# Fetching the first two samples' index pages from the stage before, by SyncE alone

## The chip, the cores and the metric

The kernel runs on one core of one Trainium2 chip. The metric is the device time of one execution in microseconds (us); lower is better. Times shown as a position ("at 1081.97") count from the first instruction of the profiled execution.

## The reference, cut to what matters

One inference step of a two-layer decoder trunk, for one prompt of 512 tokens and eight samples of one new token each, whose 2048 past tokens lie in caches cut into pages of 128 tokens. The part at hand is the indexer of layer 0, which scores the tokens and keeps the best of them; for a sample the keys of the past come through its page table:

```python
def dsa_select(qi, wi, kidx, t, topk):
    dots = jnp.einsum('bqhd,bld->bqhl', qi, kidx, preferred_element_type=jnp.float32) * (D_IDX ** -0.5)
    score = jnp.einsum('bqh,bqhl->bql', wi.astype(jnp.float32), jax.nn.relu(dots))
    s = jnp.arange(kidx.shape[1])
    score = jnp.where(s[None, None, :] <= t[None, :, None], score, NEG)
    return lax.top_k(score, topk)[1]
# in att_sample:
ki_all = jnp.concatenate([gather_pages(c_idx_k, page_table), ki], axis=1)
idx = dsa_select(qi, wi, ki_all, t, topk)
```

There are 16 index heads of 128 numbers; a sample has 16 pages of 128 x 128 float32, 64 KB each.

## The kernel before

The program is a row of stages. Each stage is a block in which every engine (TensorE, VectorE, ScalarE, GpSimd and SyncE, here PE, DVE, ACT, POOL and SP) runs its own list of instructions, ordered by semaphores. At the end of a stage GpSimd clears the stage's semaphores and all five engines meet in a barrier: the next stage starts when the last of them has come. Two stages matter here, and a third that follows.

**The prompt's block (stage_rows_and_index).** First it turns ten tiles of projections into rows for the outputs. Then it scores the prompt: a loop over the 16 index heads, two to a turn. SP fetches a head's queries into one of two buffers when the matmuls that read the buffer before are done (the DMA of line 741), PE multiplies them with the keys (line 767), ACT applies the relu (line 798), DVE adds the weighted result to the mask (line 836). Behind the loop DVE prepares the samples' queries (lines 846 to 850), and POOL cuts the mask (line 862). SP's last act in this block is one DMA of 4 MB, the weights of the next-but-one stage (load_w1, line 880), into the buffer k.w. The page table is loaded early in this block, under the semaphore table_in.

**The samples' index (stage_index_sample).** PE first clears four banks and adds the new token's own logits (lines 912 and 914); neither needs a page. Then, sample by sample, it turns the 16 pages (turn_keys, line 923, in four groups of four pages that DVE copies out, line 969), and one sample later multiplies the sample's queries with the turned keys (add_logits, line 930). So the order is: turn 0, turn 1, add 0, turn 2, add 1, turn 3 and so on. The pages lie in two buffers, of the even and the odd samples. SP fetches pages 0 to 7 of each sample and ACT pages 8 to 15, with the helper load_pages: it reads eight page numbers into registers and then issues eight DMAs of 64 KB (line 875). Ahead of each group both wait until the buffer's last sample has been turned:

```python
sp.wait_ge(turned, j * 8 + (4 * b + 4))
load_pages(k, sp, k.i["cache_dsa_idx_k"], pg[:, b, 0:8], arrived[b], j * 2 + b, 0, 8)
```

PE starts by adding 8 to the semaphore turned, so that the first two samples' fetches go at once when the stage starts. PE waits in turn_keys for all 16 pages of a sample on the semaphore arrived.

**The compression (stage_compress)** comes next; its line 1028 is the first to read the 4 MB in k.w.

Of the kernel before, what the change touches and what calls it, by code (L numbers as in the profile page):

```python
# [19 lines left out]
P = 128  # L20
# [4 lines left out]
NS = 8  # L25
# [7 lines left out]
PG = 16  # L33
# [660 lines left out]
def stage_rows_and_index(k):  # L694
# [11 lines left out]
    with ExitStack() as ctx:  # L706
# [11 lines left out]
        with nc.Block() as block:  # L718

            @block.sync  # L720
            def _(sp):
                for n, (tile, name) in enumerate(tiles):
                    if n >= 2:

                        sp.wait_ge(turned, n - 1)
                    if parts(name) == 2:
                        sp.dma_start(src[:, n % 2, :, :], k.proj[tile:tile + 2].rearrange("g p c -> p g c")).then_inc(tile_in[n % 2], 16)
                    else:
                        sp.dma_start(src[:, n % 2, 0, :], k.proj[tile]).then_inc(tile_in[n % 2], 16)
                    if n == 1:  # L730
                        sp.dma_start(k.pages[:, :], k.i["page_table"].rearrange("(o s) p -> o (s p)", o=1)).then_inc(table_in, 16)
                        sp.dma_start(k.hot[:, :], k.i["hot"][:, T:O_ALL]).then_inc(table_in, 16)
                        sp.dma_start(k.sT[:, :, :], k.proj[0:GW, :, T:TC].rearrange("t p s -> p t s")).then_inc(got, 16)
                sp.dma_start(ki[:, :], k.proj[KI]).then_inc(k_in, 16)

                sp.wait_ge(gated, 2)
                sp.dma_start(k.gate_rows, k.gws[:, :]).then_inc(out, 16)
                with sp.Fori(0, NI // 2) as j:
                    for b in range(2):
                        sp.wait_ge(mm_done, j * 2 + (b + 1))  # L740
                        sp.dma_start(q[:, b, :], k.proj[bass.ds(j * 2 + (QI + b), 1)].rearrange("o p c -> (o p) c")).then_inc(q_in[b], 16)
                load_w1(k, sp, "k")
                sp.wait_ge(table_in, 32)

            @block.tensor
            def _(pe):
# [131 lines left out]
def load_w1(k, eng, which):  # L878

    eng.dma_start(k.w1[which], k.i["cmp_w1_" + which][0].rearrange("(l d) n -> d l n", d=P)).then_inc(k.w1_in[which], 16)  # L880


def stage_index_sample(k):

    nc, ps = k.nc, k.psum
    arrived = [k.sem("is_arrived0"), k.sem("is_arrived1")]
    turned, kept, used, qcopy, relu_done, summed, scored, step = (k.sem(f"is_{n}") for n in
        ("turned", "kept", "used", "qcopy", "relu", "summed", "scored", "step"))
    with ExitStack() as ctx:
        pg = k.sb("is_pages", [P, 2, PG, P], ctx=ctx)  # L890
        kt = k.sb("is_keys", [P, 2, PAST], ctx=ctx)
        qs = k.sb("is_q", [P, 2, P], ctx=ctx)
        rl = k.sb("is_relu", [P, PAST + 1], ctx=ctx)
        sc = k.mask_s
        with nc.Block() as block:

            @block.sync
            def _(sp):
                with sp.Fori(0, NS // 2) as j:
                    for b in range(2):  # L900

                        sp.wait_ge(turned, j * 8 + (4 * b + 4))
                        load_pages(k, sp, k.i["cache_dsa_idx_k"], pg[:, b, 0:8], arrived[b], j * 2 + b, 0, 8)
                load_w1(k, sp, "v")

            @block.tensor
            def _(pe):
                pe.sem_inc(turned, 8)
                pe.sem_inc(used, 2)
                pe.sem_inc(kept, 2)  # L910
                for c in range(4):
                    pe.matmul(ps[:, c, :], k.zeros[:, :], k.xT[:, 0, 0:512], start=True, stop=True)
                for s in range(NS):
                    mm = pe.matmul(ps[:, 4, 0:1], k.qpi[:, s * P:(s + 1) * P], k.sT[:, KI, s:s + 1], start=(s == 0), stop=(s == NS - 1))
                mm.then_inc(summed, 1)

                def turn_keys(j2, s):
                    pe.wait_ge(arrived[s % 2], (j2 + s - s % 2) * (8 * PG) + 16 * PG)
                    for c in range(4):

                        pe.wait_ge(kept, j2 * 4 + (4 * s + c + 1))
                        for g in range(4):
                            mm = pe.transpose(ps[:, 5 + c % 2, g * P:(g + 1) * P], pg[:, s % 2, c * 4 + g, :], k.ident)
                        mm.then_inc(turned, 1)

                def add_logits(j2, s):
                    pe.wait_ge(qcopy, j2 + (s + 1))
                    pe.wait_ge(kept, j2 * 4 + (4 * s + 6))
                    for c in range(4):
                        mm = pe.matmul(ps[:, c, :], qs[:, s % 2, :], kt[:, s % 2, c * 512:(c + 1) * 512], start=False, stop=True, skip_group_check=True)  # L930
                    mm.then_inc(used, 1)

                turn_keys(0, 0)
                with pe.Fori(0, NS // 2 - 1) as j:
                    for s in range(2):

                        turn_keys(j * 2, s + 1)
                        add_logits(j * 2, s)
                turn_keys(0, NS - 1)
                add_logits(0, NS - 2)  # L940
                add_logits(0, NS - 1)
                pe.wait_ge(relu_done, 5)
                for c in range(4):
                    mm = pe.matmul(ps[0:NS, c, :], k.wsel[:, :], rl[:, c * 512:(c + 1) * 512], start=True, stop=True)
                pe.matmul(ps[0:NS, 4, 0:1], k.wsel[:, :], rl[:, PAST:PAST + 1], start=True, stop=True).then_inc(scored, 1)

            @block.scalar
            def _(act):
                with act.Fori(0, NS // 2) as j:
                    for b in range(2):  # L950

                        act.wait_ge(turned, j * 8 + (4 * b + 4))
                        load_pages(k, act, k.i["cache_dsa_idx_k"], pg[:, b, 8:16], arrived[b], j * 2 + b, 8, 8)
                act.wait_ge(used, NS + 2)
                act.wait_ge(summed, 1)
                for c in range(4):
                    nc.scalar.activation(rl[:, c * 512:(c + 1) * 512], ps[:, c, :], ACT.Relu).then_inc(relu_done, 1)
                nc.scalar.activation(rl[:, PAST:PAST + 1], ps[:, 4, 0:1], ACT.Relu).then_inc(relu_done, 1)

            @block.vector  # L960
            def _(dve):
                with dve.Fori(0, NS // 2) as j:
                    for b in range(2):

                        dve.wait_ge(used, j * 2 + (b + 1))
                        dve.tensor_copy(qs[:, b, :], k.qpi[:, bass.ds(j * 256 + b * P, P)]).then_inc(qcopy, 1)
                        for c in range(4):
                            dve.wait_ge(turned, j * 8 + (8 + 4 * b + c + 1))
                            dve.tensor_copy(kt[:, b, c * 512:(c + 1) * 512], ps[:, 5 + c % 2, :]).then_inc(kept, 1)
                dve.wait_ge(scored, 1)  # L970
                dve.tensor_copy(sc[:, 0:PAST], ps[0:NS, 0:4, :].rearrange("p b c -> p (b c)"))
                dve.tensor_copy(sc[:, PAST:PAST + 1], ps[0:NS, 4, 0:1]).then_inc(step, 2)
                dve.wait_ge(step, 2)
# [1419 lines left out]
def build(nc, ins, outs):  # L2393
    with ExitStack() as ctx:
        k = Kernel(nc, ctx, ins, outs)
# [13 lines left out]
        k.gate_rows = k.dram("gate_rows", [NS, NGW])  # L2409
        k.w_free = [k.sem(f"w_free{s}") for s in range(4)]  # L2410
        k.y_out = [k.sem(f"y_out{b}") for b in range(2)]
        k.w_in = [k.sem(f"w_in{s}") for s in range(4)]
        k.w1_in = {which: k.sem("w1_in_" + which) for which in "kv"}

# [4 lines left out]
        with ExitStack() as layer0:  # L2419
# [20 lines left out]
            with ExitStack() as sample:  # L2440
# [4 lines left out]
                with ExitStack() as compressing:  # L2445

                    k.w1 = {"k": k.w[:, :, :].rearrange("p s (l n) -> p (s l) n", n=CH), "v": k.sb("w1_v", [P, CB, CH], ctx=compressing)[:, :, :]}
                    with ExitStack() as indexing:
                        k.qpi = k.sb("qpi", [P, NS * P], ctx=indexing)
                        k.zeros = k.sb("zeros", [P, P], ctx=indexing)  # L2450
                        with k.stage():
                            stage_rows_and_index(k)
                        with k.stage():
                            stage_index_sample(k)
                    with k.stage():
                        stage_compress(k, "k")
                    with k.stage():
                        stage_compress(k, "v")
# [69 lines left out]
```

## Time and profile before

| what | value |
|---|---|
| time, median of 3 runs | 3264.4 us (3262.85 to 3266.66) |
| the profiled execution's own time | 3262.51 us |
| its span, first to last instruction | 3260.9 us |
| share of the span in which PE, DVE, ACT and POOL are busy | 90%, 42%, 22%, 4% |
| mean granted TensorE clock | 0.943 of full |
| prompt's scoring, first to last matmul of line 767 | 1027.1 to 1073.3 |
| samples' index, first matmul of line 912 to last of line 945 | 1081.3 to 1147.4 |

Between the end of the last instruction and what the time counts lie 1.6 us. The profile is of one execution, and the three runs lie 3.8 us apart.

### The profile page before, as it was taken

What the parts mean: (1) busy time and instruction counts of PE and PEld (TensorE: products, weight loads), DVE (VectorE), ACT (ScalarE), POOL (GpSimd) and SP (SyncE); (2) the same over time, 40 slices, a digit from 0 to 9 for tenths busy, and PEclk for the clock granted to TensorE, in tenths of its full rate; (3) what the DMA queues carried; (4) which work ended last, traced back from release to release, by engine and by line L of the source; (5) the groups of instructions that cost most, each with busy time, mean ns of one, the idle gap of its engine ahead of it and who ended that gap; (6) DMA issues with size and microseconds to landing.
All of it is one profiled execution on the core that took longest, in us unless ns stands there. A gap on an engine that the chain in (4) does not pass through costs nothing. (4 is left out here: it accounts for less than half of the span.)

```text
span 3260.9 us, 56498 instructions
## 1 busy us (share of the span) xinstructions
PE 2934.2 (90%) x22144; PEld 2601.3 (80%) x22144; DVE 1365.2 (42%) x2213; ACT 710.9 (22%) x1085; POOL 131.6 (4%) x150
## 2 busy tenths in 40 slices
PE   7699999999995789798888896797999999999897
PEld 3499999999983468688544464797999999999897
DVE  2422242222344447566562476434444334433434
ACT  2211222111221122121000254322322222222222
POOL 0000030000130000000000000000000000000000
PEclk8799999999997999899897698898999999999998
DMA  9766567676646733231889524632233333333421
GB/s 334 234 194 193 176 197 229 219 233 215 179 130 164 219 117 98 78 93 45 262 266 348 172 85 153 179 91 80 80 98 86 103 97 97 96 94 113 117 79 52
DMA packets 594874, 496.87 MB, mean 152 GB/s; under 512 B 37148, under 2 KB 515885, under 8 KB 593885
## 3 DMA queue, kind: packets, MB, share of 16 engines
q1 hardware_dynamic: 527912, 408.44, 42.5%
q10 hardware_dynamic: 58992, 60.59, 5.7%
q0 software_dynamic: 7840, 26.10, 2.1%
q8 instruction: 82, 1.34, 0.2%
q14 instruction: 48, 0.39, 0.0%
HBM read 460.02 MB, written 48.70 MB: 156 GB/s over the span
## 5 line engine op out<-in xcount | busy, mean ns | idle before, releaser
L146 PE MATMUL psum<-h_high,w_high 128*128 128x260 f32 x4992 | 1009.3, 283 | 21.6 <-DVE w_low L133 21.6
L146 PE MATMUL psum<-h_high,w_low 128*128 128x260 f32 x4992 | 1007.0, 283 | 0.0
L146 PE MATMUL psum<-h_low,w_high 128*128 128x260 f32 x4992 | 1005.2, 283 | 0.0
L146 PEld LDWEIGHTS psum<-h_high,w_high 128*128 128x128 f32 x4992 | 770.7, 189 | 35.9 <-issue 30.1
L146 PEld LDWEIGHTS psum<-h_high,w_low 128*128 128x128 f32 x4992 | 770.8, 189 | 0.0
L146 PEld LDWEIGHTS psum<-h_low,w_high 128*128 128x128 f32 x4992 | 768.9, 189 | 0.0
L133 DVE TENSOR_TENSOR w_low<-w,w_high 128x2048 fp32r<-128x2048 f32 x162 | 371.7, 2296 | 560.5 <-ACT w_high L128 560.5
L128 ACT ACTIVATE w_high<-w 128x2048 fp32r<-128x2048 f32 x162 | 309.1, 1909 | 473.3 <-PE psum L146 361.3
L628 DVE COPY pj_out<-psum 128x260 f32<-128x260 f32 x66 | 28.3, 429 | 380.3 <-PE psum L146 380.3
L576 ACT ACTIVATE pj_out<-psum 128x260 f32<-128x260 f32 x66 | 25.6, 387 | 583.3 <-PE psum L146 583.3
L199 PE MATMUL psum<-w,c 128*32 128x512 f32 x768 | 104.8, 659 | 26.1 <-DMA w<-in_w_ada 17.5
L1041 PE MATMUL psum<-w,cz_xtk 128*128 128x256 f32 x512 | 117.3, 391 | 0.0
L1041 PE MATMUL psum<-w_v,cz_xtv 128*128 128x256 f32 x512 | 117.1, 390 | 0.0
L1041 PEld LDWEIGHTS psum<-w,cz_xtk 128*128 128x128 f32 x512 | 115.4, 309 | 0.5
L1041 PEld LDWEIGHTS psum<-w_v,cz_xtv 128*128 128x128 f32 x512 | 115.3, 308 | 0.4
L1583 DVE COPY at_kt<-psum 128x512 f32<-128x512 f32 x144 | 93.0, 686 | 34.9 <-PE psum L1383 34.6
L2069 DVE TENSOR_TENSOR ou_t<-psum,adaT 128x8 f32<-128x8 f32 x32 | 5.3, 165 | 197.8 <-PE psum L146 187.0
L2351 DVE RECIPROCAL cv_parts<-cv_parts 128x520 f32<-128x520 f32 x16 | 54.5, 3404 | 71.9 <-ACT cv_parts L2285 71.9
L199 PEld LDWEIGHTS psum<-w,c 128*32 128x32 f32 x768 | 20.0, 114 | 71.3 <-issue 40.5
L166 PE MATMUL psum<-h_high,w_high 128*128 128x260 f32 x192 | 41.9, 301 | 34.2 <-DVE h_low L2036 22.4
L632 DVE RECIPROCAL pj_ez<-pj_ez 128x520 f32<-128x520 f32 x16 | 54.5, 3403 | 40.3 <-POOL pj_ez L664 40.3
L669 POOL DMA_DIRECT2D proj<-pj_out x66 | 36.7, 556 | 735.3 <-DVE pj_out L628 727.5
(372 smaller groups left out, 2772.1 us busy)
## 6 DMA issues: line engine op xcount, KB each, us to landing
w<-in_w_ada SPq DMA_DIRECT2D x96, 1024.0 KB, 7.7
w<-in_w_in_att SPq DMA_DIRECT2D x65, 1024.0 KB, 11.3
w<-in_w_in_conv SPq DMA_DIRECT2D x64, 1024.0 KB, 6.2
proj<-pj_out POOLq DMA_DIRECT2D x66, 260.0 KB, 4.8
cz_pgk<-in_cache_nsa_cmp_k SPq DMA_DIRECT2D x128, 128.0 KB, 2.1
cz_pgv<-in_cache_nsa_cmp_v SPq DMA_DIRECT2D x128, 128.0 KB, 2.1
w<-in_w_out_att SPq DMA_DIRECT2D x16, 1024.0 KB, 6.2
w<-in_w_out_conv SPq DMA_DIRECT2D x16, 1024.0 KB, 6.0
```

The lines of the kernel that those rows point to most:

```text
L128: act.activation(k.wh[:, s % 2, :], k.w[:, n % 4, :], ACT.Copy).then_inc(self.high, 1)
L133: dve.tensor_tensor(k.wl[:, s % 2, :], k.w[:, n % 4, :], k.wh[:, s % 2, :].bitcast(F32), ALU.subtract).then_inc(k.w_free[n % 4], 1)
L146: mm = pe.matmul(k.psum[:, banks + hf, 0:HC], w[:, kt, :], x[:, kt, hf * HC:(hf + 1) * HC], start=(kt == 0 and m == 0), stop=(kt == KT - 1 ...
L166: mm = pe.matmul(k.psum[:, banks[i] + hf, 0:HC], w[:, kt, :], x[:, kt, hf * HC:(hf + 1) * HC], start=(kt == 0 and m == 0), stop=(kt == KT ...
L199: mm = pe.matmul(k.psum[32 * a:32 * a + 32, self.bank, :], k.c32[:, q * 4 + a, :], k.w[:, n % 4, a * 512:(a + 1) * 512], start=(q == 0), s ...
L576: nc.scalar.activation(out[:, t % 4, 0:HC], ps[:, t % 2 * 2, 0:HC], ACT.Copy).then_inc(kept_a, 1)
L628: dve.tensor_copy(out[:, t % 4, HC:TC], ps[:, t % 2 * 2 + 1, 0:HC]).then_inc(kept_v, 1)
L632: dve.reciprocal(ez[:, t % 2, :], ez[:, t % 2, :]).then_inc(zrec, 1)
L669: pool.dma_start(to, out[:, t % 4, :]).then_inc(stored[t % 4], 16)
L1041: mm = pe.matmul(ps[:, b, 0:CH], rows, w1[:, l, :], start=(l == 0), stop=(l == CB - 1))
L1583: dve.tensor_copy(kt[:, s % 2, :, c * 256:(c + 1) * 256], ps[:, 3 + q % 2, :].rearrange("p (g q) -> p g q", g=G)).then_inc(kept, 1)
L2351: dve.reciprocal(e[:, :], e[:, :]).then_inc(zrecip, 1)
```

## The change

SP now fetches all 16 pages of samples 0 and 1 in the prompt's block: 32 DMAs in four groups, in straight-line code between its last query and load_w1, which moves behind them. The wait for the page table moves ahead of them. In the samples' stage the loops of SP and of ACT begin with the second pair of samples, so ACT fetches nothing for samples 0 and 1 any more. The page buffer is_pages and its two arrival semaphores now live across both stages.

```diff
@@ stage_rows_and_index, sync
                         sp.dma_start(q[:, b, :], k.proj[bass.ds(j * 2 + (QI + b), 1)].rearrange("o p c -> (o p) c")).then_inc(q_in[b], 16)
+                sp.wait_ge(table_in, 32)
+                for b in range(2):
+                    for half in range(0, PG, 8):
+                        load_pages(k, sp, k.i["cache_dsa_idx_k"], k.is_pages[:, b, half:half + 8], k.is_arrived[b], b, half, 8)
                 load_w1(k, sp, "k")
-                sp.wait_ge(table_in, 32)
@@ stage_index_sample
-    arrived = [k.sem("is_arrived0"), k.sem("is_arrived1")]
+    arrived = k.is_arrived
...
-        pg = k.sb("is_pages", [P, 2, PG, P], ctx=ctx)
+        pg = k.is_pages
@@ sync
-                with sp.Fori(0, NS // 2) as j:
+                with sp.Fori(1, NS // 2) as j:
@@ scalar
-                with act.Fori(0, NS // 2) as j:
+                with act.Fori(1, NS // 2) as j:
@@ build
+        k.is_arrived = [k.sem(f"is_arrived{b}") for b in range(2)]
...
+                        k.is_pages = k.sb("is_pages", [P, 2, PG, P], ctx=indexing)
```

## Rows read from the trace of the kernel before

**Rows 1.** Page, part 1: busy us (share of the span) and instructions.
```profile
PE 2934.2 (90%) x22144; PEld 2601.3 (80%) x22144; DVE 1365.2 (42%) x2213; ACT 710.9 (22%) x1085; POOL 131.6 (4%) x150
```

**Rows 2.** Timeline, all engines, 1066 to 1082: start, length, engine and line [idle before].
```profile
1065.83 2.50 SPq L741 DMA_DIRECT2D ip_q<-proj  x2
...
1068.60 4.71 PE L767 MATMUL psum<-ip_k,ip_q 128*128 128x128 f32 x16 [0.80 <-DMA ip_q<-proj]
1068.63 0.39 SPq L880 DMA_DIRECT2D w<-in_cmp_w_k  x1
...
1079.65 0.22 DVE L850 TENSOR_SCALAR wsel<-const,wi_s 128x8 f32<-128x8 f32 x1
1081.20 0.23 DVE L966 COPY is_q<-qpi 128x128 f32 x1 [1.33 <-PEq L909]
...
1081.27 1.19 PE L912 MATMUL psum<-xT,zeros 128*128 128x512 f32 x1 [7.95 <-PEq L102]
```

**Rows 3.** Timeline, PE alone, 1086 to 1101: the first three turnings.
```profile
1086.28 1.84 PE L914 MATMUL psum<-sT,qpi 128*128 128x1 f32 x16
1088.52 1.09 PE L923 MATMUL psum<-const,is_pages 128*128 128x128 f32 x8 [0.40 <-DMA is_pages<-in_cache_dsa_idx_k]
1089.96 1.25 PE L923 MATMUL psum<-const,is_pages 128*128 128x128 f32 x8 [0.35 <-DVE is_keys L969]
1093.55 1.09 PE L923 MATMUL psum<-const,is_pages 128*128 128x128 f32 x8 [2.34 <-DMA is_pages<-in_cache_dsa_idx_k]
1094.99 1.97 PE L923 MATMUL psum<-const,is_pages 128*128 128x128 f32 x8 [0.35 <-DVE is_keys L969]
1096.75 4.20 PE L930 MATMUL psum<-is_keys,is_q 128*128 128x512 f32 x8
1100.79 0.38 PE L923 MATMUL psum<-const,is_pages 128*128 128x128 f32 x2
```

**Rows 4.** Timeline, SP alone, single page fetches of samples 0, 1 and 2.
```profile
1081.97 0.34 SPq L875 DMA_DIRECT2D is_pages<-in_cache_dsa_idx_k  x1
...
1085.59 0.33 SPq L875 DMA_DIRECT2D is_pages<-in_cache_dsa_idx_k  x1
1086.84 0.33 SPq L875 DMA_DIRECT2D is_pages<-in_cache_dsa_idx_k  x1
...
1092.04 6.06 SPq L875 DMA_DIRECT2D is_pages<-in_cache_dsa_idx_k  x9
```

**Rows 5.** Timeline, SP alone, 1552 to 1574: 32 page fetches without a loop.
```profile
1554.30 8.70 SPq L875 DMA_DIRECT2D w<-in_cache_nsa_slc_k  x16
1563.73 9.94 SPq L875 DMA_DIRECT2D at_slots<-in_cache_nsa_slc_k  x16
1573.72 0.36 SPq L1296 DMA_DIRECT2D at_vn<-out_slc_v_s  x1
```

**Rows 6.** The same, single fetches: eighth of group one, first of group two.
```profile
1557.92 0.33 SPq L875 DMA_DIRECT2D w<-in_cache_nsa_slc_k  x1
1558.99 0.33 SPq L875 DMA_DIRECT2D w<-in_cache_nsa_slc_k  x1
```

**Rows 7.** DMA issues of the span: queue, count, KB each, median us to landing.
```profile
w<-in_cmp_w_k SPq DMA_DIRECT2D x1, 4096.0 KB, 15.7
is_pages<-in_cache_dsa_idx_k ACTq DMA_DIRECT2D x64, 64.0 KB, 2.3
is_pages<-in_cache_dsa_idx_k SPq DMA_DIRECT2D x64, 64.0 KB, 2.1
...
w<-in_cache_dsa_v SPq DMA_DIRECT2D x32, 128.0 KB, 9.9
```

**Rows 8.** Busy time by stretch (PE, PEld, DVE, ACT, POOL), then PE's granted clock, DMA share, GB/s.
```profile
1076.00:1080.00 4.00, 0.00 (x0) 0.00 (x0) 3.87 (x35) 0.00 (x0) 1.08 (x4) 0.69 1.10 348
1080.00:1084.00 4.00, 2.73 (x4) 1.22 (x5) 0.23 (x1) 0.00 (x0) 0.00 (x0) 0.50 0.86 267
1084.00:1086.00 2.00, 2.00 (x6) 1.01 (x5) 0.00 (x0) 0.00 (x0) 0.00 (x0) 0.92 0.90 251
1094.60:1097.90 3.30, 2.95 (x11) 2.40 (x11) 2.31 (x4) 0.00 (x0) 0.00 (x0) 0.50 0.76 218
1100.79:1106.70 5.91, 5.56 (x26) 3.18 (x25) 2.80 (x5) 0.00 (x0) 0.00 (x0) 1.00 0.54 153
```

**Rows 9.** Timeline, 1100 to 1210: the first read of the 4 MB.
```profile
1153.74 6.42 PE L1028 MATMUL psum<-w,cz_petk 128*32 128x256 f32 x64 [0.29 <-ACT cz_petk L1092]
```

## The prediction

> **What bounds the kernel now.** Read the shares of the engines first: PE is busy 90% of the span [rows 1], and no other engine half of it. The kernel is mostly a matmul stream, so time can be won or lost here only where PE stands idle, and those places are read one by one. The timeline around the seam between the two stages shows one: the last matmul of line 767 ends at 1073.31 (1068.60 + 4.71), and PE's next, of line 912, starts at 1081.27 [rows 2]. Nothing about pages holds it there. What holds it is the barrier, and the last to come is DVE, which ends line 850 at 1079.87; 1.33 us later the next stage runs. SP came long before: it ended its 4 MB issue at 1069.02. So SP has 1079.87 - 1069.02 = 10.85 us of slack in the prompt's block, and that is all the cover there is.
>
> Next, PE alone after the seam. The page waits can be seen directly: 0.40 us ahead of turn 0 and 2.34 us ahead of turn 1, both released by the fetch of is_pages [rows 3]. From turn 2 on one sample takes 5.91 us with the clock at 1.00 [rows 8], and PE waits for DVE's copies, not for pages. The whole price of the late pages is therefore 2.74 us, plus what the clock adds: the second half of turn 1 takes 1.97 us where the same of turn 0 took 1.25, and the granted clock there, 1094.6 to 1097.9, is 0.50, the lower of its two levels (1.2 GHz), after PE had stood idle from 1091.21 to 1093.55 [rows 3, 8].
>
> **The change, part by part.** *Loop bounds and semaphores.* ACT loses 16 DMAs and SP's stage-two loop 16; both engines then wait for turn 0, as they did for sample 2 before. Nothing on PE, DVE or POOL changes its own list.
>
> *The 32 fetches on SP.* First their pace. Eight fetches of one group start at 1081.97 to 1085.59, so 3.62 / 7 = 0.517 us each, and a group lasts 3.62 + 0.33 = 3.95 us [rows 4]. Then the register reads between groups: 0.92 us in the loop (1085.92 to 1086.84) [rows 4], 0.74 us in straight-line code (1558.25 to 1558.99) [rows 6]. Straight-line groups start 4.72 us apart: (1563.73 - 1554.30) / 2 [rows 5]. The change's code is straight-line, so I take 0.74 and 4.72.
>
> SP's last query issue ends at 1068.33, and 0.30 us later the old block issued its 4 MB [rows 2]. The first page then starts at 1068.33 + 0.30 + 0.74 = 1069.37; the fourth group at 1069.37 + 3 x 4.72 = 1083.53 and ends at 1087.48. The wait for the page table costs nothing, being met since the block's start. The 4 MB issue follows 0.05 us later (as line 1296 follows the pages [rows 5]) and takes 0.39: SP is done at 1087.92. DVE's end was 1079.87. **The barrier moves by 8.05 us.** Bounds: without the 0.30 and at 4.69, 7.6; if 32 fetches take 19.37 us from first to last, as those of [rows 5] did (1554.30 to 1573.67; 128 KB pages with ACT fetching too), 9.3 us.
>
> The Trainium skill, DMA: Bandwidth & Descriptors, section Issuing engines are not separate DMA queues, says that issuing from several engines saves only the sequencer's time of issue, "which is usually small relative to the DMA itself". By that word the fold onto one engine would be nearly free and the sum would be the 3.0 us of gain below. The rows disagree for this size: 32 issues at 0.517 us are 16.5 us of SP's time.
>
> *What becomes earlier after the barrier.* I count from turn 0's start, t0. Lines 912 and 914 keep their 1081.27 to 1088.12; the clock has already fallen to 0.50 at the seam [rows 8], and a longer idle time finds it no lower. Then turn 0 starts at once: 0.40 saved. Before, turn 2 started at t0 + 12.27 (1088.52 to 1100.79 [rows 3]). After, two things must be ready. PE: turn 0 takes 2.69 and turn 1 with add 0 the steady 5.91, so t0 + 8.60; or, if the clock still falls at that place, 12.27 - 2.34 = 9.93. Sample 2's pages: they can be asked for only when turn 0 is over (2.69), their first issue follows 0.83 later (1091.21 to 1092.04, [rows 3, 4]), the eighth starts 3.62 on, and 2.1 (SP) to 2.3 (ACT) later it has landed [rows 7]: t0 + 9.2 to 9.5. So **a new wait of up to 0.9 us stands ahead of turn 2** in place of the 2.34, or the lower clock does. Turn 2 starts at 9.5 or 9.9; the gain is 0.40 + 2.8, or 0.40 + 2.3: 2.7 to 3.2, I take 3.0. At best (pages no limit, no fall of the clock) it is 0.40 + 3.67 = 4.1. Sample 3 is not late: SP's next group starts at 2.69 + 0.83 + 3.95 + 0.92 = 8.4 and has landed by 8.4 + 3.62 + 2.3 = 14.3, turn 3 needs it at 9.5 + 5.91 = 15.4.
>
> *The 4 MB, moved behind 32 DMAs.* Issued at 1087.5 and not 1068.63, it lands 15.7 us later [rows 7], at 1103.2. Its reader comes at 1153.74 [rows 9], so it is not late itself. But its transfer, covered before by the prompt's last heads, now meets sample 2's fetches. With turn 0 at 1088.12 + 8.05 = 1096.2, these are issued from 1099.7 to 1103.6: the 4 MB is nearly through, and the last page, which sets the wait, is issued after it has landed. I take nothing. At worst a page lands as late as those of in_cache_dsa_v, 9.9 us [rows 7]; turn 2 then starts at 2.69 + 0.83 + 3.62 + 9.9 = 17.0, a loss of 4.7 - 0.40 = 4.3 instead of the gain.
>
> **Sum.** +8.05 - 3.0 = **+5.0 us**. Every engine passes the barrier and no later stage sees more than a shift. Bounds without a collision: 7.6 - 4.1 = +3.5 to 9.3 - 2.7 = +6.6. The profiled execution's 3262.5 (span 3260.9 and 1.6 around it) becomes 3267.5; it lies 1.9 below the median of the runs, by which it would be 3269.4. As the result is a median, I give 3269.
>
> **Rivals.**
>
> *A. The 4 MB collides* (slower). SP's sample 2 pages stand behind it in SP's own queue, while ACT's take a share of the engines. Against it: at the old seam the 4 MB's end met page fetches too, and PE still began turn 0 only 6.55 us after the first issue (1081.97 to 1088.52). For it: here it lands only about 0.4 us before the last page is issued, and 0.5 MB of ACT's pages stretch it. Three us more give +8.0, 3272.4; the worst +12.3, 3276.7. It decides when turn 2 starts 1.5 us later than 9.5, that is when the last page takes over 3.8 us to land. The same page of the Trainium skill, section Queues, rings and completion order, says that on each DMA engine descriptors are consumed in ring order, which is this rival's mechanism; no row of before shows a page fetch behind a big one in full flow.
>
> *B. SP issues slower than its best row.* The second sixteen of [rows 5] took 9.94 us; two such pairs and a 0.74 make 20.6, SP ends at 1090.4, the barrier moves 10.6, the sum is +7.6: 3272.0. Against it: that stretch had two queues with twice the bytes.
>
> *C. SP isn't what the barrier waits for* (the change does only what it says). Then the 3.0 stay, 3261.4. It needs 8 us of the issue to vanish; the slack is 10.85 and the work 32 x 0.517, so little speaks for it.
>
> **How the numbers follow.** About 0.2% (6.5 us) is what a measurement of this kernel can tell from no change. My forecast, +3.5 to +6.5, has 0.62; A 0.20 and B 0.10 lie beyond it on the slow side; C 0.06 lies within 0.2% on the other; nothing I can name reaches -6.5, 0.02. So faster 0.02, within 0.2% 0.68, slower 0.30. The range runs from 3263 (+3.5 on the profiled execution less 3 for the runs' spread, 3.8) to 3274, which takes in B and most of A; C and A's far end are left out.
>
> **What would show it.** In the profile after: SP's 32 fetches from about 1069.4 to 1087.5 and the 4 MB right behind; DVE still ending at 1079.9; PE's line 912 starting near 1089.3, its idle time before that 16 us and not 8; no page wait at turns 0 and 1; sample 2's a wait below 1 us, or the clock at 0.50 during add 0. Wrong would be: SP's groups closer than 4.7 us, a barrier before 1086, or turn 2 more than 11 us after turn 0.

## The result and the profile after

The changed kernel takes 3273.04 us in the median of 20 runs (3266.74 to 3280.14), the kernel before 3266.58 us (3261.85 to 3271.26, also 20 runs). The ratio is 1.0021, 95% interval 1.0014 to 1.0028: slower, by about 6.9 us on 3266.6, somewhere between 4.6 and 9.1. The point lies just beyond the bound of 0.2% set ahead, and the interval lies on both sides of it. The profiled execution of before, 3262.5, was 4 us quicker than that kernel's median, so spans of single profiles are not subtracted below; stretches are.

First the seam between the two stages, in the timeline of the changed kernel (all engines; line numbers have moved by three or so; `...` marks rows left out):

```profile
1065.58 0.33 SPq L741 DMA_DIRECT2D ip_q<-proj  x1
1067.13 18.00 SPq L878 DMA_DIRECT2D is_pages<-in_cache_dsa_idx_k  x32
...
1077.15 0.22 DVE L853 TENSOR_SCALAR wsel<-const,wi_s 128x8 f32<-128x8 f32 x1
1085.18 0.43 SPq L883 DMA_DIRECT2D w<-in_cmp_w_k  x1
1086.84 0.23 DVE L969 COPY is_q<-qpi 128x128 f32 x1 [9.47 <-PEq L912]
...
1086.90 1.19 PE L915 MATMUL psum<-xT,zeros 128*128 128x512 f32 x1 [16.07 <-PEq L102]
```

DVE is done at 1077.37, SP only at 1085.61, and the next stage runs 1.23 us after SP. In [rows 2] it ran 1.33 us after DVE. PE's idle time at the seam is 16.07 us where it was 7.95: the barrier costs 8.1 us more.

Then PE alone in the stage behind it (timeline of the changed kernel):

```profile
1086.90 5.50 PE L915 MATMUL psum<-xT,zeros 128*128 128x512 f32 x8 [16.07 <-PEq L102]
1092.24 1.84 PE L917 MATMUL psum<-sT,qpi 128*128 128x1 f32 x16
1093.94 1.07 PE L926 MATMUL psum<-const,is_pages 128*128 128x128 f32 x8
1095.36 1.25 PE L926 MATMUL psum<-const,is_pages 128*128 128x128 f32 x8 [0.35 <-DVE is_keys L972]
1096.80 1.25 PE L926 MATMUL psum<-const,is_pages 128*128 128x128 f32 x8 [0.19 <-DVE is_keys L972]
1098.24 1.26 PE L926 MATMUL psum<-const,is_pages 128*128 128x128 f32 x8 [0.18 <-DVE is_keys L972]
1099.33 3.60 PE L933 MATMUL psum<-is_keys,is_q 128*128 128x512 f32 x8
1103.93 1.09 PE L926 MATMUL psum<-const,is_pages 128*128 128x128 f32 x8 [1.00 <-DMA is_pages<-in_cache_dsa_idx_k]
```

Set beside [rows 3]: the page waits of 0.40 and 2.34 us are gone, and a new one of 1.00 us stands ahead of turn 2. From the clearing's first matmul to turn 2 PE takes 17.03 us (1086.90 to 1103.93); before it was 19.52.

The granted clock, by stretches of the changed kernel (the column before the DMA share), is 0.50 through the idle time, mixed while PE starts, and 1.00 through both turns; in [rows 8] it fell to 0.50 again there.

```profile
1080.00:1086.90 6.90, 0.00 (x0) 0.03 (x1) 0.06 (x1) 0.00 (x0) 0.00 (x0) 0.50 0.44 116
1086.90:1093.94 7.04, 7.04 (x24) 4.02 (x25) 0.17 (x1) 0.00 (x0) 0.00 (x0) 0.74 1.05 335
1093.94:1103.93 9.99, 8.27 (x42) 4.76 (x42) 5.52 (x10) 0.00 (x0) 0.00 (x0) 1.00 0.99 292
```

### The profile page after: what moved, and what is told of

The parts are those of the page before. It is cut to its first block and busy times, and to the rows that moved or that the text cites. A ratio compares the mean times of both kernels' runs of the same rounds, so it can differ in the third digit from the quotient of the medians.

```text
span 3270.5 us, 56485 instructions
## 1 busy us (share of the span) xinstructions
PE 2944.0 (90%) x22144; PEld 2607.5 (80%) x22144; DVE 1365.6 (42%) x2213; ACT 711.4 (22%) x1085; POOL 131.6 (4%) x150
```

## The experiments

The theory to test: SP's 32 issues make it late at the barrier (+8), and the pages that are ready give back less than that. Rivals: the 4 MB, moved behind the pages, makes the loss; or it lies in stages further down.

**1. The fetches spread between the queries.** SP's loop is written out, two pages follow each query, the rest is as in the changed kernel, against which the edit is shown (`...` marks the loop and the block of 32 that go):

```diff
-                with sp.Fori(0, NI // 2) as j:
...
+                sp.wait_ge(table_in, 32)
+                for h in range(NI):
+                    b, first = h // 8, h % 8 * 2
+                    sp.wait_ge(mm_done, h + 1)
+                    sp.dma_start(q[:, h % 2, :], k.proj[QI + h]).then_inc(q_in[h % 2], 16)
+                    load_pages(k, sp, k.i["cache_dsa_idx_k"], k.is_pages[:, b, first:first + 2], k.is_arrived[b], b, first, 2)
+                load_w1(k, sp, "k")
```

> All 32 fetches are issued by SyncE in the prompt's block, but two behind each of the 16 queries (loop written out), and the 4 MB right behind the last. If the loss is SyncE's late arrival at the barrier, it is gone: the gap of PE between the prompt's last matmul and line 912's first is 8.0 us as in the kernel before (16.1 in the changed one), no page wait at turns 0 and 1, a wait of 1.0 us or less at turn 2, 17.0 us from line 912's first matmul to turn 2 (19.5 before), and the time is 2.5 to 3 us below before, ratio 0.999. Rival, the loss sits in later stages: the gap is 8 us but the time stays 1 to 4 us above before. Third possibility: the fetches crowd the queries, 0.5 to 1 us a head in the prompt's loop, up to 10 us slower.

Measured: ratio to before 0.9987 (0.9977 to 0.9997), PE's gap at the seam 7.94 us, no page wait at turns 0 and 1, turn 2 at 18.17 us after line 912's first matmul with a wait of 1.42. All 32 fetches are still made, by SP, ahead of the barrier, and the loss is gone: it was the place of the issue, not the number of fetches. A second round of the same kernel:

> The kernel with two fetches behind each query once more, for its time and a second profile: gap 8.0 us, no wait at turns 0 and 1, turn 2 from 17.0 to 18.2 us after line 912, the time 1 to 4 us below before.

gave 0.9988 (0.9979 to 0.9997), and its timeline shows the seam, with SP done before DVE:

```profile
1067.80 0.85 SPq L876 DMA_DIRECT2D is_pages<-in_cache_dsa_idx_k  x2
...
1068.70 0.43 SPq L881 DMA_DIRECT2D w<-in_cmp_w_k  x1
...
1078.19 0.23 DVE L851 TENSOR_SCALAR wsel<-const,wi_s 128x8 f32<-128x8 f32 x1
...
1079.81 1.19 PE L913 MATMUL psum<-xT,zeros 128*128 128x512 f32 x1 [7.95 <-PEq L102]
```

The queries weren't crowded: from the start of the loop's first matmul to the start of its last the two profiles have 44.8 and 45.8 us, that of before 45.6. In both rounds this version is faster than the kernel before, by the intervals. Written out, the loop also has fixed addresses in place of computed ones; no run has that difference alone.

**2. The cost alone, with the 4 MB first.** The kernel before, and 32 fetches into a buffer that nobody reads (the buffer, its semaphores and a wait for them at the end of the next stage's SP list are left out here):

```diff
                 load_w1(k, sp, "k")
                 sp.wait_ge(table_in, 32)
+                for b in range(2):
+                    for half in range(0, PG, 8):
+                        load_pages(k, sp, k.i["cache_dsa_idx_k"], k.spare[:, b, half:half + 8], k.spare_in[b], b, half, 8)
...
```

> The kernel before, with the 32 fetches added in the prompt's block into a buffer that nobody reads, behind the 4 MB, which keeps its old place; the samples' stage still fetches all its pages itself. Issue theory: SyncE ends 32 fetches and their register reads, 18.0 us, at 7.9 us behind VectorE, the gap grows from 8.0 to 15.9 us, 19.5 us from line 912 to turn 2 as before, and the time is 8 us above before, ratio 1.0024. Rival, the moved 4 MB makes the loss: here it isn't moved, so the time stays within 1 us of before.

Measured: 1.0055 (1.0041 to 1.0069), some 18 us (13 to 23), more than twice what either theory said. PE's gap is 23.90 us. The reason is one instruction in SP's timeline, the one behind the 4 MB:

```profile
1067.92 0.39 SPq L883 DMA_DIRECT2D w<-in_cmp_w_k  x1
1069.34 7.81 SPq L878 DMA_DIRECT2D spare<-in_cache_dsa_idx_k  x1
```

The first page behind the 4 MB takes SP 7.81 us to issue, where its like take 0.33 as a rule [rows 4]. That was in neither theory, and it muddles this run as a price of 32 fetches.

**3. Sixteen fetches, the 4 MB behind them.** Sample 0 only; sample 1 at the start of its own stage, on both queues. The edit is against the changed kernel:

```diff
-                for b in range(2):
+                for b in range(1):
...
+                load_pages(k, sp, k.i["cache_dsa_idx_k"], pg[:, 1, 0:8], arrived[1], 1, 0, 8)
                 with sp.Fori(1, NS // 2) as j:
...
+                load_pages(k, act, k.i["cache_dsa_idx_k"], pg[:, 1, 8:16], arrived[1], 1, 8, 8)
                 with act.Fori(1, NS // 2) as j:
```

> SyncE fetches only sample 0's 16 pages in the prompt's block, the 4 MB behind them; sample 1's are fetched at the start of the samples' stage, half by ScalarE. Issue theory: SyncE is done at about 1076.3, 1 us before VectorE, so the gap is 8.0 us again. The 4 MB is then issued 5 us before the stage starts and is in full flow when SyncE asks for its half of sample 1. If its own queue makes these pages stand behind the 4 MB, turn 1 waits until the 4 MB has landed, 15 to 16 us after its issue, a wait of 2 to 3 us, and the time is about 0.5 us below before; if not, no wait and 2.7 us below before.

Measured: 1.0012 (1.0003 to 1.0020), slower by its interval, if by little. The gap is 7.95 us as expected, but the wait at turn 1 is 7.20 and not 2 to 3. SP's timeline shows its first fetch of sample 1, 3 us after the 4 MB:

```profile
1082.20 0.43 SPq L883 DMA_DIRECT2D w<-in_cmp_w_k  x1
1085.26 6.26 SPq L878 DMA_DIRECT2D is_pages<-in_cache_dsa_idx_k  x1
```

ACT's timeline has its eight fetches in the same microseconds:

```profile
1085.49 3.94 ACTq L878 DMA_DIRECT2D is_pages<-in_cache_dsa_idx_k  x8
```

And PE's has the wait at turn 1:

```profile
1101.52 3.70 PE L927 MATMUL psum<-const,is_pages 128*128 128x128 f32 x16 [7.20 <-DMA is_pages<-in_cache_dsa_idx_k]
```

ACT's queue goes at its own pace beside the 4 MB; SP's stands still.

**4. Sixteen fetches, the 4 MB first**, as number 3 with the two swapped:

```diff
+                load_w1(k, sp, "k")
                 sp.wait_ge(table_in, 32)
                 for b in range(1):
...
-                load_w1(k, sp, "k")
```

> As the run with sixteen fetches, but the 4 MB is issued ahead of them, at its old place. SyncE ends at about 1078, before VectorE: gap 8.0 us. Pages of sample 0 stand behind the 4 MB, landed by 1085, before turn 0 needs them; sample 1's are asked for at the stage's start with the 4 MB nearly through. No wait at turns 0 and 1 beyond 0.3 us, 1 us at turn 2, 16.9 to 17.2 us from line 912 to turn 2, the time 2.5 to 3 us below before, ratio 0.999. Rival, the 4 MB does no harm in either place: the same as the run with sixteen and the 4 MB behind.

Measured: 1.0015 (1.0006 to 1.0024), where a gain was expected. SP's timeline, single issues:

```profile
1068.84 0.39 SPq L883 DMA_DIRECT2D w<-in_cmp_w_k  x1
...
1070.27 7.98 SPq L878 DMA_DIRECT2D is_pages<-in_cache_dsa_idx_k  x1
1078.43 0.66 SPq L878 DMA_DIRECT2D is_pages<-in_cache_dsa_idx_k  x1
1079.27 0.33 SPq L878 DMA_DIRECT2D is_pages<-in_cache_dsa_idx_k  x1
...
1086.54 0.33 SPq L878 DMA_DIRECT2D is_pages<-in_cache_dsa_idx_k  x1
```

The held fetch ends at 1078.25, 9.41 us after the 4 MB was issued; in number 2 it is 9.23 (1067.92 to 1077.15), in number 3 it is 9.32 (1082.20 to 1091.52). In these three runs SP's next DMA was through only some 9.3 us after the 4 MB had been issued. PE's gap is 14.74 us, 6.8 too many, and no page is late at turns 0 and 1.

The next four take the 4 MB out of the way, with a control, and ran beside one another. All four have this edit (the compression's own SP list ends with the second 4 MB):

```diff
@@ SP's list in stage_rows_and_index
-                load_w1(k, sp, "k")
@@ end of SP's list in stage_index_sample
-                load_w1(k, sp, "v")
+                load_w1(k, sp, "k")
@@ end of SP's list in stage_compress
+                if keys:
+                    load_w1(k, sp, "v")
```

**5. The control: before, with late weights.**

> Control: the kernel before, with the 4 MB issued at the end of the samples' stage and the next stage's 4 MB at the end of SyncE's fetches for the compression. Gap 8.0 us, page waits 0.4 and 2.3 us at turns 0 and 1, 19.5 us from line 912 to turn 2; the time within 2 us of before, up to 1 us more where the compression's first small fetches meet the 4 MB.

Measured: 1.0000 (0.9992 to 1.0009): moving the 4 MB by itself costs nothing that shows (the interval is -2.6 to +2.9 us). The waits at turns 0 and 1 are 0.0 and 1.59 us, not the 0.4 and 2.3 expected, and turn 2 comes after 19.05 us.

**6. The cost alone, with late weights** (the edit of number 2 and that above).

> The 32 fetches into a buffer that nobody reads once more, but with the 4 MB out of the way: it is issued at the end of the samples' stage, and the next stage's 4 MB at the end of SyncE's fetches for the compression; the samples' stage fetches all its pages itself. Issue theory: SyncE issues from 1069.4 to 1087.4 with no fetch longer than 1.5 us, the gap of PE is 15.5 us, the page waits of turns 0 and 1 are as before (0.4 and 2.3), 19.5 us from line 912 to turn 2, and the time is 7.6 us above the control with the same late weights. Rival, most of the 18 us of the first cost run is the price of 32 more transfers and not of SyncE's queue behind the 4 MB: then this one is 15 us or more above the control too.

Measured: 1.0025 (1.0016 to 1.0034), 8.2 us over the control's 1.0000 (the interval leaves 5.2 to 11.1; the medians of the two lie 6.3 us apart). The timeline, with SP's fetches at their own pace again:

```profile
1068.54 18.21 SPq L877 DMA_DIRECT2D spare<-in_cache_dsa_idx_k  x32
...
1078.52 0.22 DVE L852 TENSOR_SCALAR wsel<-const,wi_s 128x8 f32<-128x8 f32 x1
...
1088.09 1.19 PE L916 MATMUL psum<-xT,zeros 128*128 128x512 f32 x1 [15.98 <-PEq L102]
```

SP ends 8.0 us behind DVE, and the time follows. This is the barrier's share by itself: 32 transfers that nobody uses cost what SP is late, as closely as the interval can tell. Without the 4 MB ahead no fetch stood still, so it was the 4 MB that held the first one in number 2.

**7. Sixteen fetches, with late weights.**

> Sixteen fetches in the prompt's block, sample 1's at the start of the samples' stage from both queues, and the weights late as in the control. If SyncE's queue behind the 4 MB made the 7.2 us of wait at turn 1, that wait is gone (0.3 us or less), the gap is 8.0 us, turn 2 comes 16.8 to 17.2 us after line 912, and the time is 2.5 us below the control. Rival, sample 1's pages come too late by themselves: a wait at turn 1 of 1 us or more is left.

Measured: 0.9999 (0.9990 to 1.0008), -3.3 to +2.6 us. The gap is 7.95 us and the wait of 7.20 at turn 1 is gone, so it was SP's queue behind the 4 MB. But the 2.5 us of gain are not seen: turn 2 comes 17.89 us after line 912.

**8. The changed kernel, with late weights.**

> The changed kernel with the weights late as in the control. If the 4 MB takes no part in its loss: gap 15.5 us (0.5 less, the 4 MB's own issue), no wait at turns 0 and 1, turn 2's wait still 0.8 to 1.0 us as its pages are asked for late, the time 5 us above the control. If the 4 MB's transfer is what delays sample 2's pages: that wait falls below 0.5 us.

Measured: 1.0022 (1.0013 to 1.0030), as the changed kernel itself; gap 15.95 us, the wait ahead of turn 2 still there with 1.40. So the 4 MB has no part that shows in the changed kernel's loss, nor in the wait at turn 2.

**9 and 10. Both kernels once more, for a second profile.**

> The kernel before once more, for a second profile. So far the kernels with the old fetches took 19.5, 19.1 and 17.9 us from line 912's first matmul to turn 2, those with all pages ready 16.6 to 18.2. If the spread comes from when the granted clock rises and falls again, and sample 1's pages land at a fixed place, then turn 1 starts again 12.0 to 12.3 us after line 912, and turn 2 between 17.9 and 19.5. If the 19.5 of the first profile is the rule, 19.5.

> The changed kernel once more, for a second profile: gap 16.0 us, SyncE's 32 fetches in 18.0 to 18.2 us, no wait at turns 0 and 1, a wait of 1.0 to 1.4 at turn 2, which comes 17.0 to 18.2 us after line 912.

Times of the single runs: 3264.06 and 3273.17. The first half of the second profile of before, PE's timeline:

```profile
1080.86 6.06 PE L912 MATMUL psum<-xT,zeros 128*128 128x512 f32 x8 [7.95 <-PEq L102]
...
1088.56 1.09 PE L923 MATMUL psum<-const,is_pages 128*128 128x128 f32 x8
1090.00 1.25 PE L923 MATMUL psum<-const,is_pages 128*128 128x128 f32 x8 [0.35 <-DVE is_keys L969]
1092.95 1.09 PE L923 MATMUL psum<-const,is_pages 128*128 128x128 f32 x8 [1.70 <-DMA is_pages<-in_cache_dsa_idx_k]
1094.38 1.25 PE L923 MATMUL psum<-const,is_pages 128*128 128x128 f32 x8 [0.35 <-DVE is_keys L969]
1095.47 3.60 PE L930 MATMUL psum<-is_keys,is_q 128*128 128x512 f32 x8
1098.91 1.04 PE L923 MATMUL psum<-const,is_pages 128*128 128x128 f32 x8
```

The same kernel as [rows 3], and here no wait at turn 0, 1.70 at turn 1, no slow transposes and turn 2 after 18.05 us instead of 19.52. The changed kernel's second profile has the gap at 16.14 us, SP's 32 fetches in 17.99, and turn 2 after 17.58 with a wait of 1.49.

All profiles together, in us from the first matmul of the clearing (line 912) unless said otherwise:

| kernel | gap at the seam | turn 0 starts | wait at turn 1 | turn 1 starts | turn 2 starts |
|---|---|---|---|---|---|
| before | 7.95 | 7.25 | 2.34 | 12.28 | 19.52 |
| before, again | 7.95 | 7.70 | 1.70 | 12.09 | 18.05 |
| 5: late weights | 7.95 | 7.82 | 1.59 | 12.08 | 19.05 |
| 2: cost alone | 23.90 | 7.20 | 2.12 | 12.01 | 19.31 |
| 6: cost alone, late weights | 15.98 | 7.39 | 1.91 | 11.98 | 17.94 |
| changed | 16.07 | 7.04 | 0 | | 17.03 |
| changed, again | 16.14 | 7.10 | 0 | | 17.58 |
| 8: changed, late weights | 15.95 | 7.68 | 0 | | 18.07 |
| 1: between queries | 7.94 | 7.75 | 0 | | 18.17 |
| 1, again | 7.95 | 7.08 | 0 | | 17.57 |
| 4: sixteen, 4 MB first | 14.74 | 6.63 | 0 | | 16.61 |
| 7: sixteen, late weights | 7.95 | 7.94 | 0 | | 17.89 |

The first five fetch in the old way: turn 2 starts at 18.77 in the mean. The last seven have the pages in time: 17.56. The difference of 1.2 us is uncertain by some 0.8, an estimate from the spread within the two groups. (Number 3, with its wait of 7.20, is left out.)

## Why the prediction was right, and which term was off

*The barrier, predicted +8.05: right.* The 32 issues took 18.00 us where 18.11 had been worked out from the straight-line rows, SP was done 19.70 us after its last query (1065.91 to 1085.61; worked out: 19.59), and PE's gap grew by 8.1 to 8.2. That these 8 us go into the time is shown by number 6 (8.2 over its control, 5.2 to 11.1 by its interval), and that they come from the place of the issue by number 1, where they vanish with all 32 fetches kept. One sentence of this part was too narrow: SP's 10.85 us behind its last query were not "all the cover there is", as the gaps between the queries held the 32 fetches in number 1. (The bound of 7.6 adds up to 7.7; nothing hangs on it.)

*The gain, predicted 3.0: the mechanism was right, the size was not.* Means of five and seven profiles differ by 18.77 - 17.56 = 1.2 us. The step that was mis-sized is "the gain is 0.40 + 2.8, or 0.40 + 2.3", which took one profile's 12.27 from turn 0 to turn 2 as the rule. Three things were missed. First, sample 1's pages land at a fixed place: turn 1 starts 11.98 to 12.28 us after line 912 in all five, whether turn 0 started at 7.20 or at 7.82. The wait is what is left, so when the clock rises later and turn 0 comes later, the wait shrinks by as much, and removing it gives no more than that. Second, the fall of the clock between turn 0 and turn 2 that cost the first profile over a microsecond is not in each execution. It is there in three of the five (before, numbers 2 and 5, with turn 2 at 19.05 to 19.52) and not in the other two (before again and number 6: 18.05 and 17.94, within the spread of the kernels whose pages are ready); in none of the seven does the clock fall there. From turn 0 to turn 2, before again and number 5, with the granted clock as the third number from the end:

```profile
1088.56:1098.91 10.35, 7.96 (x41) 4.94 (x41) 5.29 (x9) 0.00 (x0) 0.00 (x0) 1.00 0.69 199
1085.57:1096.80 11.23, 9.29 (x42) 6.22 (x42) 5.48 (x9) 0.00 (x0) 0.00 (x0) 0.85 0.68 193
```

By these few profiles the pages alone give 0.4 us (18.00 in the two without the fall, 17.56 in the seven), and the fall, worth 1.3 us where it comes, makes the other 0.8. Whether the wait at turn 1 brings the fall is open: it came with waits of 1.59, 2.12 and 2.34 us and not with 1.70 and 1.91. Third, what was worked out for after was too early: turn 2 began 9.95 to 10.49 us after turn 0 in the seven, not 9.5 or 9.9, with a new wait of 0.97 to 1.50 us and not 0.9, and turn 0 began 7.3 us after line 912 in the mean, where the prediction kept 6.85. Of the 1.8 us by which the gain was too large, 0.7 are the lateness of the one profile of before (19.52 against 18.77), the rest is this.

*The sum, predicted +5.0.* 8.15 - 1.2 = 6.95 by the profiles, about 6.9 by the 20 runs. That the two meet so closely is luck: the runs leave 4.6 to 9.1, which holds the forecast's 5.0 too. The forecast median, 3269, was 4.0 below the measured 3273.04; 2.2 of that is the level of before (3266.58 in 20 runs, 3264.4 in the three shown ahead), 0.4 that 3269.4 was given as 3269, the rest the gain that was taken too large. The range held the median with 1 us to spare, and its upper end had been set for rivals A and B, which did not come in the changed kernel: there the forecast had some luck. Its likeliest outcome, within 0.2% with 0.68, is just missed by the point.

*Rival A, the 4 MB collides: not in the changed kernel, but close by.* Number 8 takes the 4 MB away and nothing gets better. In numbers 2, 3 and 4 the collision is there and costs 6.8 us (the gap of 4), 7.2 (the wait of 3) and 7.9 (the gap of 2 over that of 6). What keeps the changed kernel clear is, by these numbers, distance: SP issues the 4 MB at 1085.18 and its next page at 1097.48, 12.3 us later, and the queue was held for 9.3 in the three runs. That page goes at the usual pace:

```profile
1097.48 0.34 SPq L878 DMA_DIRECT2D is_pages<-in_cache_dsa_idx_k  x1
```

The prediction placed the harm in the landing of the pages; the runs place it in SP's issue. The Trainium skill, DMA: Bandwidth & Descriptors, section Queues, rings and completion order, has descriptors consumed in ring order on each DMA engine. That a page behind the 4 MB comes late agrees with it; but the 6.26 to 7.98 us stand in SP's own instruction, and whether that page had reached a ring by then no run shows.

The sentence that "no row of before shows a page fetch behind a big one in full flow" overlooked rows that are there. In the trace of before, SP issues 259 loads of weight tiles, nearly all of 1 MB; the median issue takes 0.37 us, but 34 take over 2, the longest 7.03. And on ACT's queue the first page (128 KB) behind four loads of 512 KB takes 2.17 us (timelines of SP and of ACT):

```profile
16.67 7.03 SPq L176 DMA_DIRECT2D w<-in_w_ada  x1
...
1727.73 7.91 ACTq L1284 DMA_DIRECT2D w<-in_state_nsa_win_k  x4
1736.38 2.17 ACTq L875 DMA_DIRECT2D at_slots<-in_cache_dsa_v  x1
```

So that issues can be long behind big transfers could have been read there, ahead of numbers 2 to 4.

*Rival B*, a slower issue, did not come: 18.0 us both times. *Rival C*, a barrier that does not wait for SP, is refuted by the gap.

The Trainium skill, DMA: Bandwidth & Descriptors, section Issuing engines are not separate DMA queues, has the time of issue "usually small relative to the DMA itself". For one page of 64 KB it is a quarter, 0.517 us [rows 4] beside 2.1 us to landing [rows 7]; but it adds up on one engine: 32 issues held SP for 18.0 us, and 8 of them came through to the time.

What stays open: the kernel of number 1 is faster by 4 us in each of its two rounds, with intervals that reach down to 1; the stretches account for 1.2. Whether there is more, and where, was not found; the loop written out is one candidate, though it took no less time in the second of the two profiles. All other profiles also lose some us in the later stages against the first one of before, the same kernel's second among them (1.9 us ahead of it at line 944, 1.6 behind at the end). The most is lost by the control of number 5, 11 us from line 945 on, so nothing ties this to the change.

## What to carry to other kernels

A prefetch costs its issuing engine the time of issue, and in a kernel of stages with barriers that engine's slack at the barrier, not the idle time of the engine that waits, is what it may spend; 10.9 us of slack did not hold 18 us of issues, while the gaps between the queries of the same loop did. A wait seen in one profile is not the gain of removing it: look at what it ends on, and at what stands next (here the next sample's pages and the clock). Put a big DMA last on its queue, far ahead of the next thing that engine has to issue.

## What the runs showed of the hardware that had not been expected

The issue of a DMA of 4096 KB takes SP's instruction 0.39 to 0.43 us, but the next DMA on that queue is then held until 9.2 to 9.4 us after it, in three runs; the held instruction shows 6.26 to 7.98 us where its like show 0.33. ACT's queue isn't held meanwhile (eight issues in 3.94 us). At this place the kernel before shows nothing of it, since the next issue came 13.3 us later (1068.63 to 1081.97). At others its trace has the like, behind DMAs of 1 MB and of 512 KB (7.03 and 2.17 us, shown above).

How long PE runs at the lower clock after the seam varies from one execution to the next. From line 912's first matmul to turn 0, where no page is waited for, it took 6.60 us in number 3, at a mean granted clock of 0.79, and 7.94 us in number 7, at 0.65. It is no longer after 16 us of idle time (7.04 to 7.68) than after 8, and after 24 us it took 7.20, a page wait of 0.42 included.
